# The order in which a mixture-of-experts stage reloads its expert weights

## The chip, the cores and the metric

One core of a Trainium2 chip runs the whole program. The metric is the device time of one execution, in microseconds (us).

## The reference, cut to what matters

Two small transformer blocks run one after the other on 256 tokens of width 1024, in float32. The part that matters here stands twice, once in each layer of the second block: a mixture of 32 experts, two for each token.

```
def expert_block(args):                      # one block of rows xb, one expert e
    xb, e = args
    return (jax.nn.silu(xb @ w_gate[e]) * (xb @ w_up[e])) @ w_down[e]
...
eid = expert_id.reshape(A)                   # A = 2 * 256 assignments
order = jnp.argsort(eid)
...
return jax.ops.segment_sum(yp[dest] * w_s[:, None], tok_s, num_segments=T)
```

`w_gate[e]` and `w_up[e]` are 1024 x 512, `w_down[e]` is 512 x 1024: three matrices of 2 MiB for each expert, 192 MiB for each of the two layers.

## The kernel before

**Rounds.** The rows of an expert are laid into blocks of 32 rows (`SLOTS`). There are 48 blocks, and a round works on three of them at once (`WIDE`), on three column groups of TensorE; so a layer has 16 rounds (`ROUNDS`). The router fills blocks in the order of the experts and, while there are spare blocks, spaces the experts at one and a half blocks each (`WIDE * e // 2`), so that in most rounds the first block is of expert 2r and the other two are of expert 2r+1. The last round of both layers works on experts 30 and 31.

**A round.** Each of the three products, gate (kind 0), up (kind 1) and down (kind 2), is cut into four quarters; the semaphore `quarter_done` counts 12 of them in each round. The first block reads its expert's weights in place. For the second and third, VectorE (line 2440) and ScalarE (line 1710) first copy a quarter of the weights aside, into `side`, two quarters deep. Before the first quarter of a product is copied, VectorE waits until the first half of that kind's weights has landed for every expert up to that of the third block (`landed`), before the third quarter until the second half has (`tail_landed`). VectorE copies in the order of the quarters; the copy of the ninth, which waits for the first half of the down weights, stands ahead of the product that forms the hidden rows (line 2474). Between up and down TensorE gathers the rows of the next round (line 1196). The products are lines 1223 and 1225.

**Places.** On chip there is room for three experts (`BPE = 3`): expert e lies in place e % 3, each of its three kinds in its own part. Experts 0, 1 and 2 are loaded ahead of the stage. Every other load is issued by SyncE, in program order, through one queue. `again(e, q, kinds)` reads from a register table in which round expert e - 3 is used last, and then, for each kind asked for and each of its two halves, waits until enough quarters of that round are done and issues a transfer of 1024 KB (`put`, line 768):

```
for kind in kinds:
    for half in range(2):
        sp.wait_ge(done.sem, quarters + (done.base + 4 * kind + 2 * half))
        put(kind, e, q, half)
```

A wait holds up everything behind it on SyncE. `staggered(e, q)` is the order of the loop's body: gate of e, down of e - 1, up of e. `load_experts` is called once for each layer (lines 823 and 825), between the loads of the dense weights.

Write g, u and d for gate, up and down, and the expert's number behind it. The order of issue before is: g3 g4 u3 u4 d3 d4 g5 u5, then in a loop of eight turns g6 d5 u6, g7 d6 u7, ..., g29 d28 u29, and after the loop d29 g30 g31 u30 u31 d30 d31. A further digit is the half: g3.0 and g3.1.

Of the kernel before, what the change touches and what calls it, by code (L numbers as in the profile page):

```python
# [44 lines left out]
E = G * EPG  # L45
# [4 lines left out]
BPE = 3  # L50
# [43 lines left out]
def first_of(name):  # L94
    return next(i for i, r in enumerate(RUN) if PLAN[r][0] == name)


def count_of(name):
    return sum(PLAN[r][0] == name for r in RUN)
# [9 lines left out]
def last_dense(n, slot):  # L109

    return n - 1 - (n - 1 - slot) % RING
# [68 lines left out]
def two_blocks(nc, dram, out_x):  # L180
# [5 lines left out]
    with ctx:  # L186
# [99 lines left out]
        def after(eng, *names):  # L286

            for name in names:
                for s in st[name].values():
                    if s.n:  # L290
                        eng.wait_ge(s.sem, s.end)
# [421 lines left out]
        @block.sync  # L713
        def _(sp):
            for c in range(TC):
                sp.dma_start(x_res[:, c, :], dram["x"][c * P:(c + 1) * P, :]).then_inc(x_loaded[c], 16)

            def load(n):

                if MOE_AT[0] <= n < MOE_AT[0] + RING:  # L720
                    done = st["moe0"]["quarter_done"]
                    sp.wait_ge(done.sem, done.at(12 * (ROUNDS - 1) + 4 * (n % BPE + 1)))
                elif n >= RING:
                    sp.wait_ge(chunk_used, n - RING + 1)
                name, w = PLAN[RUN[n]]
                parts = HD if name == "cmp" else P
                sp.dma_start(ring[0:parts, n % RING, 0:w], dram["dense"][RUN[n], 0:parts, 0:w]).then_inc(slot_full[n % RING], 16)

            def load_run(n0, count):

                w, ahead = PLAN[RUN[n0]][1], RUN[n0] - n0
                whole = count // RING
                if whole and n0 < RING:
                    for u in range(RING):
                        load(n0 + u)
                    n0, count, whole = n0 + RING, count - RING, whole - 1
                if whole:
                    with sp.Fori(0, whole) as i:
                        for u in range(RING):

                            sp.wait_ge(chunk_used, i * RING + (n0 + u - RING + 1))
                            sp.dma_start(ring[:, (n0 + u) % RING, 0:w],
                                         dram["dense"][bass.ds(i * RING + (n0 + u + ahead), 1), :, 0:w]
                                         .rearrange("a p n -> p (a n)")).then_inc(slot_full[(n0 + u) % RING], 16)
                for n in range(n0 + whole * RING, n0 + count):
                    load(n)

            def loads(*names):
                for name in names:
                    n0, count = first_of(name), count_of(name)  # L750
                    if count > 2 * RING:
                        load_run(n0, count)
                    else:
                        for n in range(n0, n0 + count):
                            load(n)

            def load_experts(layer, tag, room):


                s = st["moe" + tag]  # L760
                n0 = MOE_AT[layer]
                weights = [dram["w_gate"], dram["w_up"], dram["w_down"]]
                done = s["quarter_done"]

                def put(kind, e, q, half):
                    lo = half * (CH // 2)
                    full = slot_full if half == 0 else tail_full
                    sp.dma_start(experts3[:, q, kind * CH + lo:kind * CH + lo + CH // 2],
                                 weights[kind][bass.ds(e + layer * E, 1), :, lo:lo + CH // 2]
                                 .rearrange("a p n -> p (a n)")).then_inc(full[BPE * q + kind], 16)  # L770

                def again(e, q, kinds):
                    quarters = sp.value_load(need_i[0:1, bass.ds(e - BPE, 1)], min_val=2, max_val=12 * ROUNDS)
# [5 lines that stand above are left out]
                def staggered(e, q):  # L779
                    again(e, q, (0,))  # L780
                    again(e - 1, (q + BPE - 1) % BPE, (2,))
                    again(e, q, (1,))

                if layer == 0:
                    for q in range(3 * BPE):
                        sp.sem_inc(tail_full[q], 16)
                early = sorted((last_dense(n0, BPE * q + kind), q, kind) for q in range(2) for kind in range(3))
                for n, q, kind in early:
                    sp.wait_ge(chunk_used, n + 1)
                    put(kind, q, q, 0)  # L790
                    put(kind, q, q, 1)
                after(sp, room)
                sp.wait_ge(st["ent" + tag]["squares_done"].sem, st["ent" + tag]["squares_done"].end)
                for kind in range(3):
                    put(kind, 2, 2, 0)
                    put(kind, 2, 2, 1)
                after(sp, "route" + tag)
                for kind in range(3):
                    for e in (BPE, BPE + 1):
                        again(e, e % BPE, (kind,))  # L800
                again(BPE + 2, 2, (0, 1))
                whole = (E - 2 - 2 * BPE) // BPE
                with sp.Fori(0, whole) as i:
                    for u in range(BPE):
                        staggered(i * BPE + (2 * BPE + u), u)
                assert 2 * BPE + whole * BPE == E - 2
                again(E - 3, (E - 3) % BPE, (2,))
                for kind in range(3):
                    for e in (E - 2, E - 1):
                        again(e, e % BPE, (kind,))  # L810

            for q in range(3):
                sp.sem_inc(slot_full[6 + q], 16)
            load(0)
            load(1)
            sp.dma_start(c_res[:], dram["mem"].rearrange("(c p) d -> p c d", p=P)).then_inc(mem_loaded, 16)
            for n in range(2, count_of("a_in")):
                load(n)
            loads("mem0", "cmp", "wo0", "ffn0", "b_in", "shared", "mem1", "wo1")
            after(sp, "normM1")  # L820
            sp.dma_start(c_res[:], dram["ctx"].rearrange("(c p) d -> p c d", p=P)).then_inc(ctx_loaded, 16)
            loads("ffn1", "dq", "dkv", "uqn", "uqp", "ukv", "mla_o")
            load_experts(0, "0", "mla_o")
            loads("conv_in", "conv_out")
            load_experts(1, "1", "conv_o")
            f = st["final"]
            for c in range(TC):
                sp.wait_ge(f["rows_scaled"].sem, f["rows_scaled"].at(c + 1))
                sp.dma_start(out_x[c * P:(c + 1) * P, :], x_res[:, c, :]).then_inc(stored, 16)
            sp.wait_ge(stored, 16 * TC)  # L830
# [2201 lines left out]
```

## Time and profile before

| | |
|---|---|
| median of three runs | 2174.22 us (2171.37 to 2177.16) |
| the profiled execution | 2174.22 us, its span 2172.3 us |
| mean granted TensorE clock | 0.969 |
| TensorE busy with matmuls | 2014.6 us (93%) |
| VectorE busy | 998.2 us (46%) |
| ScalarE busy | 681.6 us (31%) |
| moved by DMA | 619.87 MB, mean 285 GB/s |
| the first reload, g3.0, issued in layer 0 | 1062.05 us |
| the last expert product ends, layer 0 and layer 1 | 1529.6 and 2158.3 us |

Times in the trace count from the start of the span. Busy time of TensorE includes products that run side by side on its column groups, so a high share doesn't mean that it is at its peak. An expert stage is the stretch from some 1040 to 1530 us, and from some 1680 to 2158 us.

### The profile page before, as it was taken

What the parts mean: (1) busy time and instruction counts of PE and PEld (TensorE: products, weight loads), DVE (VectorE), ACT (ScalarE), POOL (GpSimd) and SP (SyncE); (2) the same over time, 40 slices, a digit from 0 to 9 for tenths busy, and PEclk for the clock granted to TensorE, in tenths of its full rate; (3) what the DMA queues carried; (4) which work ended last, traced back from release to release, by engine and by line L of the source; (5) the groups of instructions that cost most, each with busy time, mean ns of one, the idle gap of its engine ahead of it and who ended that gap; (6) DMA issues with size and microseconds to landing.
All of it is one profiled execution on the core that took longest, in us unless ns stands there. A gap on an engine that the chain in (4) does not pass through costs nothing.

```text
span 2172.3 us, 29479 instructions
## 1 busy us (share of the span) xinstructions
PE 2014.6 (93%) x9709; PEld 1104.7 (51%) x9710; DVE 998.2 (46%) x2209; ACT 681.6 (31%) x1085; POOL 44.3 (2%) x79
## 2 busy tenths in 40 slices
PE   8978999999899999999899978988998999898888
PEld 4534777744667776645444333433684433333333
DVE  2273888421548834444444333434415444333335
ACT  1142000010510001233455444445201555444444
POOL 2000000000000000000000000000000000000000
PEclk9879999999799999999999999999999999999999
DMA  8502898443159745221899999999654899999997
GB/s 291 180 34 79 337 348 335 175 156 147 34 199 361 289 149 193 98 97 33 333 401 422 422 412 423 422 422 410 245 193 184 357 417 422 423 422 422 422 422 280
DMA packets 78479, 619.87 MB, mean 285 GB/s; under 512 B 9632, under 2 KB 9952, under 8 KB 15664
## 3 DMA queue, kind: packets, MB, share of 16 engines
q1 hardware_dynamic: 67824, 540.51, 62.2%
q0 software_dynamic: 6912, 66.33, 8.1%
q10 hardware_dynamic: 3648, 11.89, 1.4%
q8 instruction: 44, 0.72, 0.1%
q14 instruction: 51, 0.42, 0.1%
HBM read 605.06 MB, written 13.63 MB: 285 GB/s over the span
## 4 chain that ended last, share of the span: by engine, by line
PE 67%; DMA 24%; DVE 4%; ACT 2%; issue 2%; DVEq 0%; SPq 0%; ACTq 0%
PE ps L839 26%; DMA big<-in_w_up 20%; PE ps L1049 14%; PE ps L1223 13%; PE ps L1061 7%; PE ps L853 2%; DMA big<-in_w_down 2%; PE ps L1225 2%; PE ps L1196 2%; DMA big<-in_w_gate 1%; ACT big L1710 1%; PE ps L1207 1%; DMA big<-in_dense 0%; DVE big L2105 0%; PE ps L1071 0%
## 5 line engine op out<-in xcount | busy, mean ns | idle before, releaser
L1223 PE MATMUL ps<-big,hT 128*32 128x512 f32 x3072 | 695.3, 605 | 75.4 <-ACT big L1710 65.2
L1225 PE MATMUL ps<-big,hT 128*32 x1536 | 694.5, 605 | 0.0
L1710 ACT COPY big<-big 128x1024 f32 x384 | 396.7, 1046 | 482.2 <-PE ps L1225 289.7
L2440 DVE TENSOR_SCALAR big<-big 128x1024 f32 x384 | 265.5, 693 | 513.4 <-PE ps L1225 320.9
L1223 PEld LDWEIGHTS ps<-big,hT 128*32 128x32 f32 x3072 | 188.3, 111 | 444.0 <-issue 242.6
L1049 PE MATMUL ps<-hT,big 128*128 128x256 f32 x1408 | 311.1, 379 | 0.0
L839 PE MATMUL ps<-big,hT 128*128 128x512 f32 (+4 forms) x792 | 299.1, 536 | 4.3 <-ACT hT L1651 2.3
L1049 PEld LDWEIGHTS ps<-hT,big 128*128 128x128 f32 x1408 | 266.7, 190 | 49.0 <-issue 14.8
L839 PEld LDWEIGHTS ps<-big,hT 128*128 128x128 f32 x792 | 143.5, 193 | 149.1 <-issue 140.0
L839 PE MATMUL ps<-big 64*30 64x256 f32 (+12 forms) x692 | 160.4, 519 | 21.7 <-issue 4.5
L1225 PEld LDWEIGHTS ps<-big,hT 128*32 128x32 f32 x1536 | 157.8, 111 | 4.7 <-issue 1.0
L1061 PE MATMUL ps<-big 128*128 128x512 f32 x352 | 159.2, 595 | 0.4 <-DVE big L2204 0.4
L2214 DVE SCALAR_TENSOR_TENSOR big<-big,s_ccol 128x512 f32<-128x512 f32 x196 | 147.4, 752 | 7.0
L1674 ACT ACTIVATE big<-big 128x256 f32<-128x256 f32 x44 | 18.3, 417 | 364.3 <-DVE big L2196 364.3
L839 PEld LDWEIGHTS ps<-big 128*128 128x128 f32 (+7 forms) x692 | 80.4, 198 | 84.6 <-issue 65.7
L1196 PE MATMUL ps<-big,hT 128*96 128x512 f32 x256 | 118.0, 603 | 1.2 <-DVE hT L2406 1.2
L839 PE MATMUL ps<-hT,big 128*128 128x256 f32 (+1 forms) x480 | 113.2, 398 | 1.9 <-ACT hT L1934 1.9
L839 PEld LDWEIGHTS ps<-hT,big 128*128 128x128 f32 x480 | 92.3, 192 | 23.7 <-issue 11.9
L1061 PEld LDWEIGHTS ps<-big 128*128 128x128 f32 x352 | 66.1, 190 | 72.9 <-issue 69.0
L2178 DVE TENSOR_TENSOR big<-ps,big 128x512 f32<-128x512 f32 x44 | 30.4, 690 | 117.7 <-PE ps L1049 117.0
L1196 PEld LDWEIGHTS ps<-big,hT 128*96 128x96 f32 x256 | 39.3, 163 | 78.0 <-issue 76.7
L853 PE MATMUL ps<-c_ident,big 128*128 128x128 f32 (+4 forms) x349 | 57.5, 302 | 18.3 <-DVE big L2124 11.6
(328 smaller groups left out, 1234.2 us busy)
## 6 DMA issues: line engine op xcount, KB each, us to landing
big<-in_w_down SPq DMA_DIRECT2D x128, 1024.0 KB, 21.8
big<-in_w_gate SPq DMA_DIRECT2D x128, 1024.0 KB, 23.1
big<-in_w_up SPq DMA_DIRECT2D x128, 1024.0 KB, 22.7
big<-in_dense SPq DMA_DIRECT2D x52, 1536.0 KB, 8.6
big<-in_dense POOLq DMA_DIRECT2D x28, 2048.0 KB, 10.1
big<-in_dense SPq DMA_DIRECT2D x21, 2048.0 KB, 7.8
y_rows<-c_res ACTq DMA_DIRECT2D x30, 384.0 KB, 7.0
big<-in_dense SPq DMA_DIRECT2D x5, 1024.0 KB, 7.7
```

The source lines that it names most:

```text
L839: ins = nc.tensor.matmul(out, lhsT, rhs, start=start, stop=stop)
L853: ins = nc.tensor.transpose(out, rows, const["ident"][0:k, 0:k])
L1049: ins = nc.tensor.matmul(ps[:, t % 2, f * S:(f + 1) * S], w[:, k, f * P:(f + 1) * P], hT[:, k, S:2 * S], start=k == 0, stop=k == KT - 1)
L1061: ins = nc.tensor.matmul(ps[:, 4 + 2 * c + h, :], gT[:, t % 2, c * P:(c + 1) * P], w[:, h * BW:(h + 1) * BW], start=t == 0, stop=t == FT - 1)
L1196: ins = nc.tensor.matmul(ps[0:ROWS, h, :], onehot[:, t, :], fN[:, t, h * BW:(h + 1) * BW], start=t == 0, stop=t == T - 1)
L1207: ins = nc.tensor.transpose(ps[:, h, k * ROWS:(k + 1) * ROWS], rows, const["ident"][0:ROWS, 0:ROWS])
L1223: nc.tensor.matmul(ps[g * SLOTS:(g + 1) * SLOTS, bank, :], xT[:, k, g * SLOTS:(g + 1) * SLOTS], side[:, g - 1, quarter % 2, at:at + BW], s ...
L1225: return nc.tensor.matmul(ps[0:SLOTS, bank, :], xT[:, k, 0:SLOTS], experts3[:, bass.ds(here, 1), kind * CH + row:kind * CH + row + BW] .re ...
L1710: nc.scalar.copy(side[:, 1, quarter % 2, :], experts3[:, bass.ds(there, 1), lo:lo + QW] .rearrange("p a n -> p (a n)")).then_inc(s["side2_ ...
L2178: tt(U[:, par, :, 2:S + 2], ps[:, par, :].rearrange("p (a b) -> p a b", a=2), token_scale, mult)\
L2214: ins = stt(acc, mod_w[j % 2][:, k, :], ccols[:, k, col:col + 1], acc, mult, add)
L2440: ts(side[:, 0, quarter % 2, :], experts3[:, bass.ds(there, 1), lo:lo + QW].rearrange("p a n -> p (a n)"), 1.0, None, mult).then_inc(s["si ...
```

## The change

The loads stay the same, each with the same wait; their order is different at both ends of a stage. The loop's order now begins with expert 4 and runs to expert 31: g3 u3, then g4 d3 u4, g5 d4 u5, g6 d5 u6, ..., g30 d29 u30, g31 d30 u31, then d31. The loop has nine turns instead of eight.

```
--- before.py
+++ after.py
                 after(sp, "route" + tag)
-                for kind in range(3):
-                    for e in (BPE, BPE + 1):
-                        again(e, e % BPE, (kind,))
-                again(BPE + 2, 2, (0, 1))
-                whole = (E - 2 - 2 * BPE) // BPE
+                again(BPE, 0, (0, 1))
+                whole = (E - BPE - 1) // BPE
                 with sp.Fori(0, whole) as i:
                     for u in range(BPE):
-                        staggered(i * BPE + (2 * BPE + u), u)
-                assert 2 * BPE + whole * BPE == E - 2
-                again(E - 3, (E - 3) % BPE, (2,))
-                for kind in range(3):
-                    for e in (E - 2, E - 1):
-                        again(e, e % BPE, (kind,))
+                        staggered(i * BPE + (BPE + 1 + u), (1 + u) % BPE)
+                for e in range(BPE + 1 + whole * BPE, E):
+                    staggered(e, e % BPE)
+                again(E - 1, (E - 1) % BPE, (2,))
```

## Rows read from the trace of the kernel before

**Rows 1.** The page: head, DMA in 40 slices, the chain by line.
```profile
span 2172.3 us, 29479 instructions
...
DMA  8502898443159745221899999999654899999997
...
PE ps L839 26%; DMA big<-in_w_up 20%; PE ps L1049 14%; PE ps L1223 13%; PE ps L1061 7%; PE ps L853 2%; DMA big<-in_w_down 2%; PE ps L1225 2%; PE ps L1196 2%; DMA big<-in_w_gate 1%; ACT big L1710 1%; PE ps L1207 1%; DMA big<-in_dense 0%; DVE big L2105 0%; PE ps L1071 0%
```

**Rows 2.** The chain in time, end of layer 1: start us, us, what.
```profile
2085.53 26.68 DMA big<-in_w_up
...
2122.54 3.60 PE ps L1196 x8
...
2130.55 17.76 DMA big<-in_w_down
...
2149.25 0.67 DVE hT L2474
...
2158.25 5.36 PE ps L839 x12
```

**Rows 3.** Windows; behind the engines' busy time: granted clock, DMA share, GB/s.
```profile
1065.00:1120.00 55.00, 53.78 (x338) 24.14 (x337) 24.43 (x44) 30.30 (x34) 0.00 (x0) 1.00 1.00 395
1120.00:1200.00 80.00, 78.31 (x489) 31.56 (x483) 34.50 (x60) 41.57 (x47) 0.00 (x0) 1.00 1.01 422
1200.00:1480.00 280.00, 248.71 (x1476) 107.12 (x1476) 106.88 (x189) 126.79 (x144) 0.00 (x0) 0.96 1.01 420
1697.00:1756.00 59.00, 57.77 (x370) 22.85 (x364) 26.23 (x46) 33.66 (x38) 0.00 (x0) 1.00 1.00 401
```

**Rows 4.** Timeline of SyncE, start of layer 0: start us, us, issues merged.
```profile
1062.05 5.20 SPq L768 DMA_DIRECT2D big<-in_w_gate  x4
1068.92 6.52 SPq L768 DMA_DIRECT2D big<-in_w_up  x4
...
1073.37 0.33 SPq L768 DMA_DIRECT2D big<-in_w_up  x1
...
1081.46 7.07 SPq L768 DMA_DIRECT2D big<-in_w_down  x4
...
1086.10 2.42 SPq L768 DMA_DIRECT2D big<-in_w_down  x3
1089.77 3.76 SPq L768 DMA_DIRECT2D big<-in_w_gate  x2
```

**Rows 5.** Line 768, the one issue g3.0, and its time to landing.
```profile
L768 SPq DMA_DIRECT2D big<-in_w_gate x1: 333/333/333, 1062.1 to 1062.1; - x1
...
DMA to landing us min/median/max: 5.0/5.0/5.0
```

**Rows 6.** The same for d30.0, in layer 0 and in layer 1.
```profile
L768 SPq DMA_DIRECT2D big<-in_w_down x1: 327/327/327, 1489.9 to 1489.9; - x1
...
DMA to landing us min/median/max: 22.9/22.9/22.9
...
L768 SPq DMA_DIRECT2D big<-in_w_down x1: 328/328/328, 2123.6 to 2123.6; - x1
...
DMA to landing us min/median/max: 18.9/18.9/18.9
```

**Rows 7.** The chain in time, end of layer 0.
```profile
1456.70 23.57 DMA big<-in_w_up
...
1488.89 3.60 PE ps L1196 x8
...
1496.90 21.20 DMA big<-in_w_down
...
1529.57 5.36 PE ps L839 x12
```

**Rows 8.** Windows over the last down products of layer 0, columns as in rows 3.
```profile
1516.00:1521.00 5.00, 0.97 (x7) 0.84 (x10) 2.48 (x5) 1.99 (x2) 1.43 (x2) 0.98 0.94 330
1521.00:1530.00 9.00, 9.00 (x49) 3.69 (x45) 4.74 (x8) 2.10 (x2) 0.00 (x0) 0.82 0.08 31
```

## The prediction

> **What bounds the kernel now.** I read the page first: its head, its slices, its chain [rows 1]. The reader should look at the DMA slices: they stand at 9 from the twentieth to the twenty-seventh and again over the last seven whole ones. Those are the two expert stages. Loads of `in_w_up` alone hold 20% of the chain, so TensorE is not what bounds these stages, at least not all through. Second, the chain in order of time [rows 2]: late in layer 1 it runs from the landing of an `in_w_up` half into a short stretch of products and back to the issue of another such half. Third, the windows [rows 3]: from 1120 us on the queue moves 422 GB/s without a break. A half of 1.049 MB then costs 2.49 us, an expert's six halves 14.9 us, and two experts, which is what a round uses up, 29.8 us.
>
> So an expert stage has two regimes. While the three resident experts and their successors are ahead, TensorE sets the pace; from about round 5 on, the stream of weights does. In the second regime only two things move the end: transfer time that the queue lost at the start and can't win back, and what the last round still has to do when its last weights land.
>
> **The change, part by part.** No byte, product or copy goes or comes; 174 half-loads of each layer are issued in another order, and the order from g6 to u29 (g, u, d: gate, up, down; the number is the expert) is the same but for its first and last neighbours. Before: g3 g4 u3 u4 d3 d4 g5 u5 | g6 d5 u6 ... d28 u29 | d29 g30 g31 u30 u31 d30 d31. After: g3 u3 g4 d3 u4 g5 d4 u5 | the same | g30 d29 u30 g31 d30 u31 d31. SyncE makes as many register reads in both orders (seven up to u5, seven behind u29), so they cost nothing; the step from one expert's issue to the next, read included, is about 1 us (1086.10 + 2.42 less two issues and their steps holds it, [rows 4]).
>
> *Start.* SyncE waits in order, each half for the quarter of a product that frees its place [rows 4]: g3.0 at 1062.05, u3.0 at 1068.92, u3.1 at 1073.37, d3.0 at 1081.46, g5.0 at 1089.77; d3.1 at 1086.10; the two halves of one gate come 3.4 us apart (3.76 less 0.33 in the last row; g3.1 so at 1065.5). Before, g4 goes right behind g3, since expert 1 leaves in the same round 0 as expert 0. After, g4 stands behind u3.1 (1074.4), u4 behind d3.1 (1087.1), d4 behind g5.1 (1094.2). Nothing in rounds 1 and 2 waits for them: g4 would land near 1081 us, and round 2, which works on it, begins after 1110: g5.0, which waits for round 1, goes 27.7 us after g3.0, which waits for round 0, and one such step more is 1117. What is lost is queue time. A half that finds the queue empty lands 5.0 us after its issue [rows 5], so its bytes begin about 2.5 us after it. After the change (a half begins at its issue + 2.5 or at the end of the one before, whichever is later, and takes 2.49): g3.0 ends at 1067.1, g3.1 begins 0.9 us later, u3.0 1.0 us after g3.1's end, u3.1 2.0 us after that of u3.0; g4 follows back to back to 1083.3; d3.0 begins 0.6 us late, d3.1 2.1 us; from u4 on something is always queued. Idle: 6.6 us. Before, the windows tell it [rows 3]: 395 instead of 422 GB/s over 55 us is 3.5 us lost in layer 0, and 401 over 59 us is 2.9 us in layer 1. After the change the later part of that loss is filled, since the queue is some 5 us deep from 1096 us on, so I count the 6.6 us alone. Layer 1's stage is issued against the same waits. Net lag of the stream: 3.1 us in layer 0, 3.7 us in layer 1, 6.8 us. Bounds, for each layer: 1.8 us if bytes begin 0.2 to 0.3 us earlier after an issue at each of the five gaps; 4.4 us if part of the 2.9 to 3.5 us is no idleness but slow transfers that stay. So 3.6 to 8.8 us. A gain would need the idle time of before to vanish whole; that is a rival below.
>
> *Does the lag reach the end?* Its cover would be a stretch in which the queue runs empty anyway. From 1120 to 1480 us it moves 422 and 420 GB/s [rows 3], and the chain's long pieces are loads. So it goes through one to one.
>
> *End.* Seven loads of two halves, 5.0 us each, follow u29 in both orders. d31 is last in both. u31 moves from fifth to sixth place, g31 from third to fourth, d29 from first to second: each 5 us later; g30 and u30 come earlier, which is worth nothing, as the last round works on 30 and 31 at once and its copies wait for the later one. Hence u31.0 takes the place that d30.0 has now: 1489.92 + 22.9 = 1512.8 us in layer 0, 2123.55 + 18.9 = 2142.5 us in layer 1 [rows 6]. From the landing of an up half to the end of the up products takes 8.6 us in layer 0 (1456.70 + 23.57 = 1480.3, to 1488.89, where the next rows' gathering L1196 begins, [rows 7]) and 10.3 us in layer 1 (2085.53 + 26.68 = 2112.2 to 2122.5, [rows 2]). From the start of the hidden rows, 0.25 us later, to the last product it is 9.0 us (2149.25 to 2158.25, [rows 2]). With 8.6: layer 0 ends at 1512.8 + 8.6 + 9.25 = 1530.7 instead of 1529.6 us, +1.1; layer 1 at 2142.5 + 17.85 = 2160.4 instead of 2158.25, +2.1. With 10.3: +2.8 and +3.8. I take 8.6, since the slower one had its second half late. Sum 3.2 (to 6.6) us, on top of the lag. Why so little of 5 us: in layer 0 the last round now waits for d31.0 (lands at 1496.90 + 21.20 = 1518.1, [rows 7]) after its up products are done, and that wait shrinks; in layer 1 the last round has slack all through. g31 is no wait: u31.0 lands 10 us after g31.0, and one product takes 8.6. d29, 5 us later, may hold up round 14's down products by 1 to 2 us, which the wait for u31 swallows.
>
> The Trainium skill, "DMA: Bandwidth & Descriptors", section "Where 436 GB/s comes from", says that HBM allows a core about 358 GB/s; this trace shows 422 GB/s for 80 us on end [rows 3]. By the page's figure two halves would cost 5.9 instead of 5.0 us and u31 would come 5.9 us later in each layer instead of 5.0 (an estimate from that page). The measurement decides.
>
> Sum: 6.8 + 3.2 = 10.0 us. The profiled execution took 2174.22 us (span 2172.3), which is also the median, so: 2184.2 us.
>
> **Rivals.**
> *The lag is absorbed* (chance 0.22). Early landings before may be slow for reasons of their own, or the stream has idle spots in layer 0's middle. Against it: 420 GB/s over 1200 to 1480. Then only the tails are left: 2174.2 + 3.2 = 2177.4 us.
> *The orders are equivalent* (0.07): if the last round's end were set by d31 alone, both would be hidden, 2174 us. Against it: in layer 1 d31.0 lands at 2130.55 + 17.76 = 2148.3 us, and the hidden rows begin at 2149.25 [rows 2], so the last up products had no slack to give for 5 us.
> *Faster* (0.05): if the queue, fuller from 1087 us on, took back the 3.5 and 2.9 us that the windows show lost, and the 6.6 us of gaps did not arise (transfers that overlap their start-up under the waits), the stream would gain 6.4 us: 2174.2 - 6.4 + 3.2 = 2171.0 us, and 2167.8 us if the tails cost nothing; for a result that is told from no change it takes a little of both, so that case stands for about 2167 us. It decides where the gaps of a layer stay under 1.3 us, and u3.1's wait until 1073.37 alone makes 2.0.
> *The clock* (0.10). After the pause in front of d31 TensorE was granted 0.98 and then 0.82, that is, its lower level (1.2 of 2.4 GHz) for part of the stretch [rows 8], and from d31.0's landing to the end it took 11.5 us in layer 0 (1518.1 to 1529.6) against 9.9 us in layer 1. The new order moves the pause in front of the up products. If the clock falls there, each layer pays some 1.6 us: 10.0 + 3.2 = 13.2, 2187.4 us. The Trainium skill, "TensorE: Matmul & The Clock Gate", section "What's actually happening", says that the throttled state is the default and that activity lifts it; by it a pause can cost, as that row shows, though what it costs is taken from these rows.
>
> **How the numbers follow.** Both terms as worked out 0.56, clock 0.10, absorbed 0.22, equivalent 0.07, faster 0.05. The likeliest has 2184.2; its own range is 2174.2 + 3.6 + 3.2 = 2181.0 to 2189.6 (8.8 + 6.6). For 8 in 10 the range takes in absorbed and clock: 2177 to 2189. About 0.3% (6.5 us) is what the measurement tells from no change. Above 2180.7 lie the clock and nearly all of the likeliest: 0.63. Below 2167.7: 0.04, nearly all of the faster case. The rest, 0.33, is the same.
>
> **What would show it.** In the trace after: the issue of g4 some 12 us after that of g3.0, not among the four gate issues of one 5.2 us; landings of u3.1 and d3.1 within 5.2 us of issue, and GB/s under 350 twice before 1090; from there the landing of any half of experts 7 to 28 about 3 us later relative to g3's issue; the last round's waits on an `in_w_up` half instead of `in_w_down`. The prediction is wrong if landings in mid-stage stand where they stood (no lag), or if the last round still waits on d31. It would also be wrong if round 2 waited for g4 or d4 (a bigger loss), which 30 us of margin makes unlikely.

## The result, and the profile after

| | before | after |
|---|---|---|
| median | 2174.93 us (2171.37 to 2178.30, 5 runs) | 2188.58 us (2180.96 to 2189.82, 5 runs) |
| profiled execution | 2174.22 us | 2190.59 us |
| ratio after to before | | 1.0059, 95% interval 1.0039 to 1.0080 |

The kernel is slower by 13.65 us at the medians. That is inside the predicted range (2177 to 2189), 0.4 us below its upper end, and clear of the 0.3% that tells from no change. The profiled execution shows 16.4 us; below it turns out that 12.6 of them lie in the two expert stages and the rest ahead of both.

The page of the changed kernel, its head, its DMA slices and the chain by line (compare [rows 1]; lines of the program stand five lower from here on, so L1218 and L1220 are the products, L1191 the gathering, L834 the work that follows a stage):

```profile
span 2188.7 us, 29543 instructions
...
DMA  8501899443159744311899999999655899999996
...
PE ps L834 26%; DMA big<-in_w_up 24%; PE ps L1044 14%; PE ps L1218 11%; PE ps L1056 7%; PE ps L1220 2%; PE ps L848 2%; PE ps L1191 1%; ACT big L1705 1%; DMA big<-in_w_gate 1%; DMA big<-in_dense 0%; PE ps L1202 0%; DVE big L2100 0%; DMA big<-in_w_down 0%; PE ps L1066 0%
```

Loads of `in_w_up` went from 20% of the chain to 24%, the products L1218 from 13% to 11%, `in_w_down` from 2% to nothing. More of the stage is spent on the stream, and the last round no longer waits for a down weight.

SyncE's timeline at the start of layer 0 (compare [rows 4]):

```profile
1065.89 3.77 SPq L768 DMA_DIRECT2D big<-in_w_gate  x2
1072.82 4.73 SPq L768 DMA_DIRECT2D big<-in_w_up  x2
1078.51 0.95 SPq L768 DMA_DIRECT2D big<-in_w_gate  x2
1085.45 4.97 SPq L768 DMA_DIRECT2D big<-in_w_down  x2
1091.17 0.84 SPq L768 DMA_DIRECT2D big<-in_w_up  x2
1093.78 3.75 SPq L768 DMA_DIRECT2D big<-in_w_gate  x2
```

g3 and u3 stand where they stood, counted from g3.0; g4 comes 12.6 us after g3.0, u4 25.3 us. Before, both were out by 12.7 us. Between 1079.5 and 1085.4 us SyncE has nothing it may issue, though expert 4's up place has been free as long as expert 3's.

The windows show what that does. The first two are short; the other three span nearly the same stretches, counted from g3.0, as the first, second and last of [rows 3] (columns as there: the last is GB/s):

```profile
1070.00:1075.00 5.00, 4.34 (x33) 2.06 (x28) 1.53 (x3) 4.22 (x5) 0.00 (x0) 1.00 0.87 279
1075.00:1080.00 5.00, 5.00 (x23) 1.99 (x17) 1.98 (x3) 2.68 (x3) 0.00 (x0) 1.00 0.69 238
1069.00:1124.00 55.00, 53.83 (x337) 25.14 (x337) 24.49 (x43) 30.32 (x34) 0.00 (x0) 1.00 0.94 368
1124.00:1204.00 80.00, 76.97 (x480) 32.09 (x477) 34.28 (x60) 41.34 (x47) 0.00 (x0) 1.00 1.01 423
...
1706.00:1765.00 59.00, 57.77 (x367) 22.92 (x364) 26.39 (x47) 33.69 (x38) 0.00 (x0) 1.00 0.95 370
```

368 instead of 422 GB/s over 55 us is 7.0 us lost, where it was 3.5 [rows 3]; 370 over 59 us is 7.3, where it was 2.9. After that the queue runs at 423 GB/s (422 before): what is late by then stays so but for 0.5 us. Against the kernel before, counted from g3.0, the landings of experts 11 to 20 come 3.5 us later in layer 0 and 5.3 us in layer 1 (medians over the 60 halves), and those of experts 21 to 28 3.5 and 5.4 us. The lag is not constant from the start: expert 5's halves are late by 5.2 us in layer 0 and 5.7 in layer 1 (medians), expert 10's by 3.4 and 5.3. So part of the first loss is won back in layer 0 and little of it in layer 1.

The chain at the end of layer 0 and of layer 1 (compare [rows 7] and [rows 2]):

```profile
1461.89 26.00 DMA big<-in_w_up
...
1493.12 26.41 DMA big<-in_w_up
1519.68 1.05 ACT big L1705
...
1529.88 0.10 DVE hT L2469
...
1538.81 5.36 PE ps L834 x12
```

```profile
2100.12 26.70 DMA big<-in_w_up
...
2133.74 23.32 DMA big<-in_w_up
2157.22 1.05 ACT big L1705
...
2174.62 5.36 PE ps L834 x12
```

In both layers the last wait is for u31.0, which lands at 1519.5 and 2157.1 us. Up products follow, hidden rows, down products. From g3.0's issue (1703.35 us in layer 1) to the last product it is 472.9 and 471.3 us, against 467.5 and 464.1 us before: +5.4 and +7.2, 12.6 us in all. The stretch between the stages and what follows the second take as long as before, within 0.1 us. The other 3.8 us of the profiled execution came before the first g3.0, which went at 1065.89 instead of 1062.05 us.

### The profile page after: what moved, and what is told of

The parts are those of the page before. It is cut to its first block, busy times and chain, and to the rows that moved or that the text cites. A ratio compares the mean times of both kernels' runs of the same rounds, so it can differ in the third digit from the quotient of the medians.

```text
span 2188.7 us, 29543 instructions
## 1 busy us (share of the span) xinstructions
PE 2024.3 (92%) x9709; PEld 1110.9 (51%) x9710; DVE 997.6 (46%) x2209; ACT 680.8 (31%) x1085; POOL 45.5 (2%) x79
## 4 chain that ended last, share of the span: by engine, by line
PE 65%; DMA 26%; DVE 4%; ACT 2%; issue 2%; DVEq 0%; SPq 0%; ACTq 0%
PE ps L834 26%; DMA big<-in_w_up 24%; PE ps L1044 14%; PE ps L1218 11%; PE ps L1056 7%; PE ps L1220 2%; PE ps L848 2%; PE ps L1191 1%; ACT big L1705 1%; DMA big<-in_w_gate 1%; DMA big<-in_dense 0%; PE ps L1202 0%; DVE big L2100 0%; DMA big<-in_w_down 0%; PE ps L1066 0%
## 5 line engine op out<-in xcount | busy, mean ns | idle before, releaser
L1218 PE MATMUL ps<-big,hT 128*32 128x512 f32 x3072 | 702.0, 609 | 85.9 <-ACT big L1705 74.4
L1220 PE MATMUL ps<-big,hT 128*32 x1536 | 701.1, 609 | 0.0
L1218 PEld LDWEIGHTS ps<-big,hT 128*32 128x32 f32 x3072 | 189.1, 112 | 454.6 <-issue 242.7
L834 PE MATMUL ps<-big,hT 128*128 128x512 f32 (+4 forms) x792 | 299.8, 537 | 4.7 <-DMA big<-in_dense 2.4
L834 PEld LDWEIGHTS ps<-big,hT 128*128 128x128 f32 x792 | 144.0, 194 | 149.6 <-issue 140.3
L834 PE MATMUL ps<-big 64*30 64x256 f32 (+12 forms) x692 | 161.0, 521 | 21.6 <-issue 5.5
L1220 PEld LDWEIGHTS ps<-big,hT 128*32 128x32 f32 x1536 | 159.0, 112 | 5.6 <-issue 0.2
L834 PEld LDWEIGHTS ps<-big 128*128 128x128 f32 (+7 forms) x692 | 79.2, 195 | 86.1 <-issue 68.2
L1191 PE MATMUL ps<-big,hT 128*96 128x512 f32 x256 | 117.6, 602 | 1.2 <-DVE hT L2401 1.2
L834 PE MATMUL ps<-hT,big 128*128 128x256 f32 (+1 forms) x480 | 114.3, 400 | 1.9 <-ACT hT L1929 1.9
L834 PEld LDWEIGHTS ps<-hT,big 128*128 128x128 f32 x480 | 93.1, 194 | 24.0 <-issue 11.9
L1191 PEld LDWEIGHTS ps<-big,hT 128*96 128x96 f32 x256 | 39.1, 162 | 77.6 <-issue 76.2
## 6 DMA issues: line engine op xcount, KB each, us to landing
big<-in_w_gate SPq DMA_DIRECT2D x128, 1024.0 KB, 24.5
```

What stands on the lines that cost most here:

```text
L834: ins = nc.tensor.matmul(out, lhsT, rhs, start=start, stop=stop)
L1191: ins = nc.tensor.matmul(ps[0:ROWS, h, :], onehot[:, t, :], fN[:, t, h * BW:(h + 1) * BW], start=t == 0, stop=t == T - 1)
L1218: nc.tensor.matmul(ps[g * SLOTS:(g + 1) * SLOTS, bank, :], xT[:, k, g * SLOTS:(g + 1) * SLOTS], side[:, g - 1, quarter % 2, at:at + BW], s ...
L1220: return nc.tensor.matmul(ps[0:SLOTS, bank, :], xT[:, k, 0:SLOTS], experts3[:, bass.ds(here, 1), kind * CH + row:kind * CH + row + BW] .re ...
```

## The experiments

All of them change the kernel before, unless said otherwise. Short names: the *lag* is how much later (+) or earlier (-) the halves of experts 11 to 20 land than in the profiled execution before (a median, counted from g3.0's issue); *end* is the same for the last product of the stage. Both are read from one profiled execution of each kernel. The ratio comes from all its timed runs; it is not the quotient of the two medians given below, and differs from it by up to 0.0007.

| | lag, layer 0 / 1 | end, layer 0 / 1 | ratio (95%) |
|---|---|---|---|
| the change | +3.5 / +5.3 | +5.4 / +7.2 | 1.0059 (1.0039 to 1.0080) |
| e1 new start | +3.4 / +5.3 | +3.4 / +6.2 | 1.0044 (1.0030 to 1.0058) |
| e2 new end | +0.5 / +0.4 | +2.1 / +2.2 | 1.0011 (0.9998 to 1.0023) |
| e3 worse start | +8.4 / +10.1 | +7.6 / +12.7 | 1.0080 (1.0065 to 1.0094) |
| e6 u4 early | +0.3 / +2.0 | -0.1 / +2.9 | 1.0009 (0.9995 to 1.0023) |
| e5 g4 first | +3.5 / +4.9 | +3.7 / +4.9 | 1.0039 (1.0024 to 1.0053) |
| e4 end, u31 early | +0.7 / +0.9 | +0.3 / +0.8 | 0.9993 (0.9982 to 1.0005) |
| e12 two moves back | +0.4 / +1.9 | 0.0 / +2.9 | 1.0013 (1.0002 to 1.0024) |
| e10 the change again | +3.9 / +5.4 | +5.8 / +7.2 | 1.0052 (1.0038 to 1.0067) |
| e7 hidden rows first | +1.0 / +0.5 | +0.2 / +2.4 | 0.9992 (0.9981 to 1.0004) |
| e9 halves in turn | -1.6 / 0.0 | -2.5 / +2.6 | 0.9992 (0.9981 to 1.0004) |
| e8 both of these | -1.5 / -0.4 | -2.5 / -1.0 | 0.9973 (0.9960 to 0.9985) |
| e11 e8 again | -1.5 / -0.1 | -4.1 / -0.9 | 0.9972 (0.9960 to 0.9984) |

The lags of e2, e4 and e7, whose start is the old one, are 0.4 to 1.0 us where nothing differs: so much is chance of one execution. The execution they are counted from was itself early. Against the mean of the four executions with the old start (before, e2, e4, e7) the change's lags are 2.9 and 4.9 us, e10's 3.3 and 4.9, e6's -0.3 and +1.5, e11's -2.1 and -0.5. An end also holds TensorE's clock in the last rounds: the last down products took 7.2 us where the clock stayed at 1.00, and 8.2 to 9.8 us where its mean was 0.87 to 0.72.

### e1: the new start alone

```
-for kind in range(3):
-    for e in (BPE, BPE + 1):
-        again(e, e % BPE, (kind,))
-again(BPE + 2, 2, (0, 1))
+for e, kind in ((3, 0), (3, 1), (4, 0), (3, 2), (4, 1), (5, 0), (4, 2), (5, 1)):
+    again(e, e % BPE, (kind,))
```

> The new order at the start of a stage alone (g3 u3 g4 d3 u4 g5 d4 u5), the old one at its end (d29 g30 g31 u30 u31 d30 d31). The changed kernel's own trace has landings of experts 7 to 28 late by 3.4 us in layer 0 and 5.3 us in layer 1, counted from the issue of g3.0. Theory (the queue runs dry while SyncE waits, and the lost time is never won back): the same lags here, and the last product of each stage late by about the same, 3.4 and 5.3 us, so 8.7 us in all, some 2183.5 us. Rival (the start only moves landings that nobody waits for, the end of the order is what costs): lags in mid-stage, but under 1 us at the last product, no change in time.

The loop is the old one. Measured: 2185.04 us against 2175.27, ratio 1.0044. Lags +3.4 and +5.3, ends +3.4 and +6.2 us. The lag goes through to the end nearly one to one, so the rival (lags that nobody waits for) falls. The start is the larger part of the loss. The window at the same place as above shows 370 GB/s:

```profile
1063.74:1118.74 55.00, 53.78 (x338) 23.88 (x337) 24.41 (x44) 30.29 (x34) 0.00 (x0) 1.00 0.94 370
```

### e2: the new end alone

```
-again(E - 3, (E - 3) % BPE, (2,))
-for kind in range(3):
-    for e in (E - 2, E - 1):
-        again(e, e % BPE, (kind,))
+for e, kind in ((30, 0), (29, 2), (30, 1), (31, 0), (30, 2), (31, 1), (31, 2)):
+    again(e, e % BPE, (kind,))
```

> The old order at the start, the new one at the end (g30 d29 u30 g31 d30 u31 d31). Theory (u31 is one place later in the stream, and the last round waits for it): no lag in mid-stage (within 0.5 us), the last product late by about 2 us in each layer, so 3 to 4 us in all, 2178 us, within 0.3%. Rival (the end carries most of the loss, since the last round can't hide a load that comes 5 us later): 5 us in each layer, 10 us in all, 2185 us.

Measured: 2178.66 us against 2175.27, ratio 1.0011. Less the lag, the last product is late by 1.6 and 1.8 us, not by 5 as the rival has it. The time alone doesn't tell it from no change; the trace does. The ratios of e1 and e2 make 1.0055 together, close to the whole change's 1.0059. In the chain the last wait is for u31.0 in both layers, here in layer 1:

```profile
2122.03 23.33 DMA big<-in_w_up
...
2162.92 5.36 PE ps L836 x12
```

### e3: a dose

```
+for e, kind in ((3, 0), (3, 1), (3, 2), (4, 0), (4, 1), (4, 2), (5, 0), (5, 1)):
+    again(e, e % BPE, (kind,))
```

in place of the lines taken out in e1.

> A dose: at the start g3 u3 d3 g4 u4 d4 g5 u5, so that all of expert 4 stands behind the last wait of expert 3; the end is the old one. Theory: by the same arithmetic of issues and transfers the queue is dry until d3.1 is out, and landings from expert 7 on are late by 7.5 to 9 us in each layer, the time longer by 15 to 18 us, about 2191 us. Rival (any departure from the old order costs a fixed amount, by code or by the loop): the lag stays at 3 to 5 us and the time near 2184 us.

Measured: 2193.79 us against 2175.27, 18.5 us, ratio 1.0080, with lags of +8.4 and +10.1 us, the second a little over the range. A fixed price for leaving the old order is out. Layer 1's end, +12.7, is 2.6 us beyond its lag: the last down products took 9.8 us there, at a mean clock of 0.72, instead of 7.2. The timeline shows all of expert 4 behind d3.1, and the window what the queue lost, 331 GB/s, or 11.9 us of 55:

```profile
1070.08 4.78 SPq L768 DMA_DIRECT2D big<-in_w_up  x2
1082.61 4.97 SPq L768 DMA_DIRECT2D big<-in_w_down  x2
1088.20 1.86 SPq L768 DMA_DIRECT2D big<-in_w_gate  x2
1090.72 0.81 SPq L768 DMA_DIRECT2D big<-in_w_up  x2
```

```profile
1066.16:1121.16 55.00, 53.77 (x338) 24.16 (x337) 24.42 (x44) 30.29 (x34) 0.00 (x0) 1.00 0.86 331
```

Three kernels give three points in layer 0: lost in the window beyond what was lost before, 3.5 us (the change), 3.3 (e1), 8.4 (e3); lag in mid-stage, 3.5, 3.4, 8.4. Bytes that have not moved by the end of the window are bytes that land late, so what this shows is that nothing of it is won back behind the window; that the dry queue is the cause rests on e3, e5 and e6, where the order of the waits alone changes. In layer 1 the account doesn't close: 4.3, 4.1 and 8.8 us lost beyond before (370, 372 and 338 GB/s over the 59 us) against lags of 5.3, 5.3 and 10.1 us. Where the other 1.0 to 1.3 us come from is open.

### e6: u4 out of the way of d3's wait

```
-for e, kind in (..., (4, 0), (3, 2), (4, 1), ...):     # e1
+for e, kind in (..., (4, 0), (4, 1), (3, 2), ...):
```

> As the new start, but u4 ahead of d3 (g3 u3 g4 u4 d3 g5 d4 u5), so that it doesn't stand behind the wait of d3.1; g4 still stands behind u3.1; the end is the old one. Theory: about 2.7 us less of dry queue than with the new start in each layer, a lag of 0.8 us in layer 0 and 2.6 us in layer 1, in all 3.4 us, about 2178 us. Rival (the late g4 makes the loss): lags as with the new start, 3.4 and 5.3 us, about 2183.5 us.

Measured: 2178.81 us against 2175.27, ratio 1.0009. Lags +0.3 and +2.0 us, each 3.1 to 3.3 us less than in e1. One load moved by one place takes back most of the start's loss:

```profile
1073.81 0.80 SPq L768 DMA_DIRECT2D big<-in_w_gate  x2
1075.30 0.82 SPq L768 DMA_DIRECT2D big<-in_w_up  x2
1080.96 4.97 SPq L768 DMA_DIRECT2D big<-in_w_down  x2
```

u4 goes at 1075.30, 13.8 us after g3.0, ahead of the wait of d3.

### e5: g4 back in its old place, u4 not

```
-for e, kind in ((3, 0), (3, 1), (4, 0), ...):     # e1
+for e, kind in ((3, 0), (4, 0), (3, 1), ...):
```

> Start g3 g4 u3 d3 u4 g5 d4 u5, end as before the change: g4 keeps its old place right behind g3, u4 and d4 stand where the change puts them. Theory (only dry queue counts, and up to d3.1 the same eight halves go out whether g4 is early or late, with the last of them released at the same moment): the lag stays at that of the whole new start, 3.4 us in layer 0 and 5.3 us in layer 1, about 2184 us. Rival (each expert-4 load that comes late costs a part of its own): the lag falls by about a third or more, to 2.2 and 3.5 us.

Measured: 2185.88 us against 2176.76, ratio 1.0039; lags +3.5 and +4.9 us. g4's early place is worth nothing as long as u4 stands behind d3.1: up to and with d3.1 eight halves go out, and they are the same eight. The new start sends three loads of expert 4 late: g4, u4 and d4 (behind g5.1). d4 is late in e6 too, where layer 0's lag is gone, so in layer 0 u4 alone costs.

### e4: the new end with u31 early

```
+for e, kind in ((30, 0), (29, 2), (30, 1), (31, 0), (31, 1), (30, 2), (31, 2)):
+    again(e, e % BPE, (kind,))
```

in place of the lines taken out in e2.

> Start as before the change, end g30 d29 u30 g31 u31 d30 d31: g31 and d29 5 us later as in the change, but u31 back in fifth place. Theory (the last round waits for u31 alone): the last product of each stage within 0.5 us of before, counted from the issue of g3.0, no change in time, 2175 us. Rival (d29 or g31, late by one place, cost as well): 1 us or more late in each layer, about as with the whole new end (2.1 and 2.2 us).

Measured: 2175.31 us against 2176.76, ratio 0.9993; ends +0.3 and +0.8 us, no more than the lag of that execution (+0.7 and +0.9). g31 and d29 a place later cost nothing that shows.

### e12: the change with those two moves taken back

Both orders of e6 and e4 in one kernel; the loop is again the one of the kernel before.

> The change with two of its moves taken back: u4 ahead of d3 at the start (g3 u3 g4 u4 d3 g5 d4 u5) and u31 ahead of d30 at the end (g30 d29 u30 g31 u31 d30 d31). Theory (u4 behind d3.1 and u31 behind d30 are most of the loss): lags in mid-stage of 0.3 us in layer 0 and 2.0 us in layer 1, the last product late by the same and no more, 2 to 3 us in all, ratio 1.000 to 1.002. Rival (the loss is spread over all moved loads): half or more of it stays, 6 us, ratio 1.003.

Measured: 2177.16 us against 2174.97, ratio 1.0013, 2.2 us where the change has 13.65. In layer 0 nothing is left, in layer 1 2.9 us, as in e6. Most of it comes with g4 behind u3.1's wait and not with d4: when u4.1 lands, ahead of d4's place, e6 is already late by 1.8 us in layer 0 and 2.3 in layer 1 (26.3 and 26.2 us after g3.0 instead of 24.5 and 23.9). Layer 0 wins that back by expert 10, layer 1 doesn't. How much of the rest is chance isn't known. u4 and u31 carry three quarters or more of the loss.

### e10: the change again

The changed kernel, unedited, in another set of runs.

> The changed kernel once more, beside before on the same chip, to see what of its profiled 16.4 us repeats. Theory (12.5 us lie in the two expert stages, 3.8 us came before g3.0 of layer 0 and are chance of one execution): in the stages, lags of 5.4 and 7.1 us at the last product, within 1 us; the issue of the first g3.0 anywhere from 1060 to 1066 us; a ratio of 1.005 to 1.006. Rival (the loop's code moves the rest of the program): the first g3.0 late by 3 to 4 us again, a ratio of 1.0075.

Measured: 2185.88 us against 2174.85, ratio 1.0052. Ends +5.8 and +7.2 us: the 12.6 us in the stages repeat to 0.4 us. The first g3.0 goes at 1060.24 us, earlier than before the change. Over the fourteen profiled executions of this study it goes between 1060.2 and 1066.1 us, in kernels with the old start too (1066.07 in e4): that part is chance.

### e7: hidden rows ahead of the ninth copy

```
-for j in range(9):
+for j in range(8 if last else 9):
     copy(b, there, loads, j, first)
...
-copy(b, there, loads, 9, first)
+for j in range(8 if last else 9, 10):
+    copy(b, there, loads, j, first)
```

> The order before the change; in the last round alone VectorE forms the hidden rows ahead of the copy of the ninth quarter, so that they no longer stand behind the wait for d31.0. Theory (in layer 0 that wait is the last one, in layer 1 it has 0.3 us of slack): the last product 1 to 1.5 us earlier in layer 0, 0 to 0.5 us in layer 1, about 2173.5 us. Rival (the copies set the pace, not the hidden rows): no difference.

Measured: 2174.74 us against 2176.76, ratio 0.9992, not told from no change. Layer 0: end +0.2 with a lag of +1.0, so 0.8 us won, a little under the 1 to 1.5 expected. Layer 1: +2.4 with +0.5, so 1.9 us lost, a miss. The ninth copy had run beside the last up products there and now comes after them, so the last down products began 2.4 instead of 2.1 us after the up products. TensorE's mean clock behind that was 0.87 and 0.85, where it had been 1.00, and the down products took 8.9 instead of 7.2 us, which is 1.7 of the 1.9:

```profile
2148.00:2152.00 4.00, 2.65 (x15) 1.62 (x18) 2.42 (x5) 1.99 (x2) 3.44 (x3) 0.87 0.85 291
2152.00:2160.00 8.00, 8.00 (x45) 3.88 (x40) 4.83 (x7) 2.27 (x3) 0.00 (x0) 0.85 0.46 177
```

### e9 and e8: a start with less dry queue, alone and with e7's edit

```
 for kind in range(3):
-    for e in (BPE, BPE + 1):
-        again(e, e % BPE, (kind,))
+    for half in range(2):
+        for e in (BPE, BPE + 1):
+            again(e, e % BPE, (kind,), (half,))     # one half of a kind
...                                             # again takes the halves as its last argument
```

> A version meant to beat both: the last round as in the run before this one, and at the start the halves of experts 3 and 4 in turn (g3.0 g4.0 g3.1 g4.1 u3.0 u4.0 ...), since those of one kind and half are released by the same quarter. Theory (less dry queue, won once and kept): landings from expert 7 on 0.7 to 1.8 us earlier than before the change in each layer; with the last round, 2 to 5 us less in all, about 2171.5 us. Rival (the old order has no dry queue left to win at the start): mid-stage landings within 0.3 us, time as in the run before this one.

> The halves of experts 3 and 4 in turn at the start, and nothing else changed; the last round as before the change. Theory (the gain of the run with both edits came from the start; moving the hidden rows cost 1 us in layer 1, where the ninth quarter's copy had been hidden): mid-stage landings earlier by 0.4 to 1.5 us, the last product earlier by about as much in each layer, time 0.1 to 0.3% below before, about 2171 to 2174 us. Rival (the gain came from the last round): no difference from before.

> The version that beat the kernel before, once more beside it: halves of experts 3 and 4 in turn at the start, hidden rows ahead of the ninth copy in the last round. The two edits alone gave 0.9992 each. Theory (it is worth what its trace shows, 2.5 us in layer 0 and 1.0 us in layer 1): ratio 0.998 to 0.9985. Rival (the first measurement of it was right to the digit): 0.9973 or below.

Measured: e9 2172.44 us against 2174.85, ratio 0.9992 (0.9981 to 1.0004), which is not told from no change and short of the 0.1 to 0.3% expected. e8 2169.32 us against 2176.76, ratio 0.9973; once more (e11), 2168.79 us against 2174.97, ratio 0.9972 (0.9960 to 0.9984). The pair repeats: a version faster than the kernel before by about 0.3%. The window of e8, at the same place again, has 401 GB/s where it was 395:

```profile
1068.55:1123.55 55.00, 53.77 (x338) 24.08 (x337) 24.41 (x44) 30.27 (x34) 0.00 (x0) 1.00 0.99 401
```

In layer 0 the lag is -1.5 or -1.6 in all three; in layer 1 it is 0.0 to -0.4, less than expected. e9's layer 1 ended 2.6 us late for another reason, the clock, at 0.75 under its last down products:

```profile
2141.00:2146.00 5.00, 2.38 (x15) 1.12 (x12) 2.62 (x5) 1.99 (x2) 3.57 (x4) 0.82 0.93 302
2146.00:2156.00 10.00, 10.00 (x50) 3.85 (x45) 4.70 (x6) 2.14 (x3) 0.00 (x0) 0.75 0.32 120
```

My expectation for e11 (0.998 to 0.9985, what e8's trace showed in the stages) was too small: in its profiled execution e11's stages are 4.1 and 0.9 us shorter, 5.0 us where the medians differ by 6.2. Of layer 0's 4.1, 1.6 us more than in e8, the clock explains nearly all: the same last down products of the same kernel took 8.7 us in e8 and 7.2 us in e11. The windows over them, e8 and then e11:

```profile
1522.00:1531.00 9.00, 9.00 (x49) 3.55 (x50) 4.78 (x9) 2.10 (x2) 0.00 (x0) 0.83 0.38 141
...
1521.00:1529.00 8.00, 7.41 (x49) 3.63 (x50) 5.34 (x11) 2.89 (x3) 0.43 (x1) 1.00 0.49 180
```

Two edits of 0.9992 each make 0.9984 together; their intervals hold 0.9972 as well. Whether the edits help each other stays open.

## Why the prediction was right, point by point

*The regime.* Right. The stream bounds a stage once the ramp is over, and from expert 11 on nothing is won back: 423 GB/s after the change, 422 before. (In the page the DMA slices at 9 are the twenty-first to the twenty-eighth, not the twentieth to the twenty-seventh; nothing hangs on it.)

*The start.* Right in kind, too small in size. I counted 6.6 us of gaps for the queue; the windows show 7.0 and 7.3 us lost. From that I took off 3.5 and 2.9 us and had a lag of 3.1 and 3.7 us; measured, it is 3.5 and 5.3 us (3.9 and 5.4 in e10). So the first term of the sum, 6.8 us, measured 8.8 (7.7 against the mean of the executions with the old start); layer 1 lies over the bound of 4.4 that I gave for one layer. The step that was too simple is the 2.9 and 3.5 us that I took off, as if the new order won back all that the old one had lost later in the ramp. Layer 0 wins back 1.8 us of expert 5's lag by expert 10, layer 1 0.4. Why layer 1 wins back less wasn't tried. Of the causes I named, g4 behind u3.1 and u4 behind d3.1, the second carries nearly all of it in layer 0 (e6, e5).

*The lag reaches the end.* Right (e1, e3).

*The end.* Right: the last round waits for u31.0. The second term, 3.2 us, measured 3.7 in the trace of the change (5.4 less 3.5, 7.2 less 5.4) and 3.4 in e2; the change's ends less e1's give 3.0. One reason that I gave was wrong. I put the slower of the two rows, 10.3 us from an up half's landing to the end of the up products, down to a late second half. That half, u29.1, landed 2.9 us behind u29.0 there and 3.4 us in the faster stretch. It was the clock: 0.84 from 2112 to 2123 us, where the other stretch, 8.6 us, had 1.00.

```profile
1480.00:1489.00 9.00, 7.26 (x49) 3.27 (x50) 3.84 (x7) 5.62 (x6) 0.00 (x0) 1.00 1.02 425
2112.00:2123.00 11.00, 9.33 (x50) 4.63 (x51) 4.18 (x8) 5.96 (x7) 0.00 (x0) 0.84 1.02 424
```

(These two windows are of the kernel before.) After the change the same two durations come back with the layers exchanged: 10.2 us in layer 0 at 0.82 and 8.5 us in layer 1 at 1.00, while the down products now run at full clock in both:

```profile
1520.70:1530.00 9.30, 9.13 (x50) 4.43 (x50) 3.99 (x10) 4.72 (x7) 4.18 (x4) 0.82 0.79 278
1530.00:1539.00 9.00, 8.21 (x55) 4.39 (x54) 6.25 (x12) 3.03 (x3) 0.00 (x0) 1.00 0.10 42
2157.00:2166.00 9.00, 7.53 (x50) 3.48 (x50) 5.11 (x12) 5.93 (x7) 4.08 (x4) 1.00 0.51 161
```

So the clock rival was half right: the fall moved from the down products to the up products in layer 0 and did not come in layer 1. Against the kernel before, which had its fall too, that is no new price. But my sum had the clock at full in both: 17.85 us from u31.0's landing to the last product. It took 19.3 us in layer 0 and 17.6 in layer 1; u31.0 itself landed 0.6 us earlier in layer 0 than its place and the lag give, which hid part of that. The pauses ahead of the last up products were not the same, 3.11 us of standing still in layer 0 and 1.80 in layer 1 (3.15 and 1.80 in e10, with the same outcome):

```profile
1520.87 0.62 PE L1218 MATMUL ps<-big,hT 128*32 128x512 f32 x2 [3.11 <-ACT big L1705]
...
2158.41 0.62 PE L1218 MATMUL ps<-big,hT 128*32 128x512 f32 x2 [1.80 <-ACT big L1705]
```

That TensorE stands throttled by default and is let up by activity, as the Trainium skill has it ("TensorE: Matmul & The Clock Gate", "What's actually happening"), agrees with the falls coming after a pause. A pause alone doesn't decide it: the last down products of e8 and e11 differ by 1.5 us at the same place of the same kernel.

*The sum.* 10.0 us were predicted. The stages show 12.6 (13.0 in e10), the medians 13.65 (11.0 in e10). The mechanism and the direction are right and both terms are somewhat small; that 2188.58 still lies inside the stated range, 0.4 us below its end, has some luck in it. The likeliest case's own range, 2181.0 to 2189.6, holds 2188.58.

*The rivals.* "The lag is absorbed" falls with e1. "The orders are equivalent" falls with the chain, which ends in `in_w_up`. "Faster" would have needed gaps under 1.3 us a layer; the windows show 7.

*The signs I named.* g4 12 us after g3.0: 12.6. GB/s under 350 twice before 1090: 279 and 238. The wait of the last round on `in_w_up`: yes. Landings of u3.1 and d3.1 within 5.2 us of their issue: u3.1 5.2 and 5.0, d3.1 5.4 and 6.6, so the second not.

*The rate.* The page "DMA: Bandwidth & Descriptors" of the Trainium skill ("Where 436 GB/s comes from") has 358 GB/s as what HBM allows a core; no run here agrees, 423 GB/s stood for 80 us on end after the change too.

## What to carry to other kernels

When a stage is bound by one stream of loads, look at the first moments in which it could run: time that the queue stands dry there, less what it wins back before the ramp is over, comes back nearly one to one at the end, and the way to see it is the mean GB/s of a window over the ramp, against the rate of the steady part. In a queue issued in order, a load that is released early must not stand behind one that is released late; here one load of two halves behind one such wait cost 3 us in each layer (e1 against e6). At the other end, what counts is how much work is left when the last load of each kind lands, so the kind that starts the longest chain of work should come first, not the expert that comes first.

## What the runs showed of the hardware that I had not expected

- A half issued into an empty or nearly empty queue landed in 4.8 to 5.5 us in most cases here. d3.0 in the changed kernel took 7.1 us (7.3 in layer 1): it landed 26.7 us after g3.0's issue, while the half ahead of it had landed at 22.2, so neither its own 5 us nor a queue explains it. The trace of that issue:

```profile
L768 SPq DMA_DIRECT2D big<-in_w_down x1: 333/333/333, 1085.4 to 1085.4; - x1
...
DMA to landing us min/median/max: 7.1/7.1/7.1
```

  It is no chance of one execution: e10, the same kernel, had 6.9 and 7.6 us there. In e1, e3 and e5, which issue d3 ahead of the loop and find the queue as empty, it took 4.9 to 5.4 us; the changed kernel issues it as the second load of the loop. Whether the loop is the cause wasn't tried. It costs little: with the same start e1 had nearly the same lag in mid-stage.
- The stretch ahead of the first expert stage varies by 6 us between executions (g3.0 at 1060.2 to 1066.1 us) with no edit in it, as much as half of what the change costs. Only a comparison stage by stage told the 12.6 us of the change from it.
- The pause of TensorE in a last round was followed by a lower mean clock (0.71 to 0.87 over 8 to 10 us) in some executions and by 1.00 in others, once at the same place of the same kernel (e8 and e11, layer 0: 0.83 and 1.00). The last down products took 7.2 us or 8.2 to 9.8 us by it, a difference the size of the effects that e7 and e9 were made to find.
